# Sixteen chunk sums of a modulation vector, moved from a Hyena block into the attention's projections

## What is computed

```python
sh1, sc1, g1, sh2, sc2, g2 = jnp.split((silu(c) @ w_mod + b_mod), 6)          # 6 x 1024 numbers
csh1, csc1, ...            = jnp.split((silu(c_ctx) @ w_mod + b_mod), 6)      # only csh1, csc1 are used
h  = modulate(rms_norm(x, norm1_g), sh1, sc1)       # 1024 positions
hc = modulate(rms_norm(ctx, norm1_g), csh1, csc1)   # 256 positions
y  = token_mixers(h, hc, ...)     # Hyena, attention A (4 heads), differential attention D (4 heads), output projection
x  = x + g1 * y
h  = modulate(rms_norm(x, norm2_g), sh2, sc2)
x  = x + g2 * conv_glu(h, ...)
```

## Time and profile before

| what | value |
|---|---|
| runs (3) | 4012.69, 4017.70, 4017.53 us; median 4017.53 |
| profiled execution, its own time | 4013.59 us |
| span of its trace | 4012.3 us, so 1.3 us lie around it |
| TensorE busy, mean granted clock | 3562.4 us (89%), 0.965 |
| VectorE busy | 1372.2 us (34%) |
| ScalarE busy | 904.3 us (23%) |
| GpSimd busy | 245.5 us (6%) |
| first block's Hyena | about 181 to 443 us of the span |
| attention's projections | about 444 to 774 us |
| moved by DMA | 362.23 MB, mean 90 GB/s |

### The profile page before, as it was taken

How to read it: one execution, slowest core, us unless ns; L and a number is a source line. 1 busy time by engine, 2 the same in 40 slices (tenths; PEclk the granted TensorE clock), 3 DMA queues, 4 the chain that set the end, 5 groups by cost and what they waited for, 6 DMA issues and landing times.

```text
span 4012.3 us, 30603 instructions
## 1 busy us (share of the span) xinstructions
PE 3562.4 (89%) x12486; PEld 1958.2 (49%) x12486; DVE 1372.2 (34%) x2502; ACT 904.3 (23%) x1725; POOL 245.5 (6%) x236
## 2 busy tenths in 40 slices
PE   8797799888888899999999999999789978999991
PEld 4356454766664344444444456665356434444440
DVE  6758344166661211111100013224556141111116
ACT  1210245256662200000000012112334131111112
POOL 0002001000000000000000000000000002222213
PEclk9898999999999999999999999999999988999996
DMA  4225200000002111011011100002000118888874
GB/s 176 74 99 205 84 23 30 22 1 1 1 1 84 42 42 42 32 42 39 29 36 36 62 32 27 32 10 84 11 1 22 44 49 333 330 329 329 332 291 152
DMA packets 59784, 362.23 MB, mean 90 GB/s; under 512 B 6442, under 2 KB 12858, under 8 KB 33020
## 3 DMA queue, kind: packets, MB, share of 16 engines
q1 hardware_dynamic: 37036, 179.39, 12.3%
q0 software_dynamic: 22608, 180.89, 12.2%
HBM read 325.03 MB, written 35.22 MB: 90 GB/s over the span
## 4 chain that ended last, share of the span: by engine, by line
PE 75%; DVE 14%; ACT 8%; issue 2%; DMA 1%; POOL 0%; SPq 0%; DVEq 0%; ACTq 0%; POOLq 0%
PE ps L1154 15%; PE ps L2245 8%; PE ps L1201 8%; PE ps L1310 5%; PE ps L2262 4%; PE ps L764 4%; ACT arena L961 3%; PE ps L1904 3%; PE ps L1099 3%; PE ps L1312 3%; PE ps L664 2%; PE ps L767 2%; ACT arena L953 2%; PE ps L603 1%; PE ps L1744 1%
## 5 line engine op out<-in xcount | busy, mean ns | idle before, releaser
L1154 PE MATMUL ps<-arena 128*128 128x512 f32 x1408 | 606.3, 593 | 5.0 <-ACT arena L1140 5.0
L1154 PEld LDWEIGHTS ps<-arena 128*128 128x128 f32 x1408 | 268.1, 190 | 343.0 <-issue 337.3
L2245 PE MATMUL ps<-arena 128*128 128x512 f32 x752 | 332.0, 594 | 0.0
L1201 PE MATMUL ps<-arena 128*128 128x512 f32 x704 | 302.4, 591 | 1.4 <-DVE arena L1187 1.4
L2203 POOL DMA_INDIRECT arena<-in_wgu_dram,arena x47 | 44.2, 940 | 2837.7 <-DVE arena L2164 2593.0
L2245 PEld LDWEIGHTS ps<-arena 128*128 128x128 f32 x752 | 139.7, 191 | 159.1 <-issue 159.1
L2262 PE MATMUL ps<-arena 128*128 128x512 f32 x376 | 174.0, 605 | 48.6 <-DVE arena L2313 48.6
L1201 PEld LDWEIGHTS ps<-arena 128*128 128x128 f32 x704 | 132.8, 189 | 171.0 <-issue 168.8
L1310 PE MATMUL ps<-arena 128*128 128x512 f32 x480 | 210.6, 599 | 0.0
L764 PE MATMUL ps<-arena 128*128 128x512 f32 (+1 forms) x432 | 174.8, 558 | 7.8 <-DMA arena<-in_win_a_dram 7.8
L911 PE MATMUL ps<-arena 128*128 128x128 f32 x1280 | 163.1, 283 | 5.4 <-ACT arena L953 2.5
(11 more groups left out here) (331 smaller groups left out, 4697.3 us busy)
## 6 DMA issues: line engine op xcount, KB each, us to landing
arena<-in_wmod_dram SPq DMA_DIRECT2D x24, 1024.0 KB, 4.9
yslot<-arena SPq DMA_DIRECT2D x47, 512.0 KB, 7.8
arena<-in_wup_dram SPq DMA_DIRECT2D x22, 1024.0 KB, 4.9
arena<-in_wout_dram SPq DMA_DIRECT2D x16, 1024.0 KB, 4.8
arena<-in_cf_dram SPq DMA_DIRECT2D x12, 1024.0 KB, 5.0
arena<-in_wdn_dram SPq DMA_DIRECT2D x16, 704.0 KB, 4.1
arena<-in_w2b_dram SPq DMA_DIRECT2D x9, 1024.0 KB, 5.0
arena<-in_ci_dram SPq DMA_DIRECT2D x8, 1024.0 KB, 6.9
```

Source lines behind the costliest of these rows:

```text
L1154: ins = mm(bk(b + tc), sb(wat(n) + k * 256 + which * 128, 128), sb(HT + k * 1024 + tc * 512, 512), k == 0, k == 7)
L1201: ins = mm(bk(bs[tc]), sb(wat(n) + k * 128, 128), sb(GB + (11 * hh + k) * 1024 + tc * 512, 512), hh == 0 and k == 0, hh == 1 and k == 10)
L2245: ins = mm(bk(b), sb(XB + i % 2 * 1024 + k * 128, 128), sb(WGU[i % 3] + k * 512, 512), k == 0, k == 7)
```

## The change

Three things: the 16 late chunks leave the ring of weights, and get a buffer `WM` of 1 MB with a semaphore `lmod`; the calls of the three steps leave Hyena and stand in the loop over the 57 jobs, with their sums behind iteration i for i in `mod_at`, TensorE's step two iterations later and the bias three later; and `AMUL2` is made behind that loop. `WM` lies on memory that Hyena's transforms use, so its first load waits for Hyena's end. TensorE's step uses PSUM bank 7 for these chunks.

```diff
-WLIST = ([("cz", 1), ("wmod", 4)] + [("cf", 1), ("wmod", 1)] * 4 + [("win_hy", 1), ("wmod", 1), ("win_hy", 1), ("wmod", 2), ("win_hy", 1), ("wmod", 2)]
-         + [("cf", 1), ("wmod", 1)] * 4 + [("ci", 1), ("wmod", 1)] * 4 + [("cf", 1), ("wmod", 1)] * 3 + [("cf", 1)] + [("ci", 4)]
+WLIST = ([("cz", 1), ("wmod", 4)] + [("cf", 1), ("wmod", 1)] * 4 + [("win_hy", 3)]
+         + [("cf", 4), ("ci", 4)] * 2
...
+    WM = BIG + 31168
+    lmod = nc.alloc_semaphore("late_mod")
+    def mbank_of(i):
+        return 6 if i < 8 else 7
...
     def dve_mod_sums(i):
-        n = nth["wmod"][i]
+        w = wat(nth["wmod"][i]) if i < 8 else WM
         V.wait_ge(*(yield ("silu",)))
-        V.wait_ge(*wready(n))
+        V.wait_ge(*(wready(nth["wmod"][i]) if i < 8 else (lmod, 16 * (i - 7))))
...
-        at[("macc", i)] = at[("w", n)] = V.last()
+        at[("macc", i)] = V.last()
+        if i < 8:
+            at[("w", nth["wmod"][i])] = V.last()
...
     def pe_conv(o):
...
-            if (o, kt) < (1, 3):
-                yield from pe_mod_step(5 + 8 * o + kt)
...
-            if o == 0:
-                yield from pe_mod_step(9 + t)
...
     def dve_conv(o):
...
-            if (o, kt) < (1, 3):
-                yield from dve_mod_step(5 + 8 * o + kt)
...
-            if o == 0:
-                yield from dve_mod_step(9 + t)
...
     def pe_hyena():
...
                 yield from pe_hy_turn(f - 1)
-                yield from pe_mod_step(f - 1)
...
-        yield from pe_mod_step(16)
...
     def dve_hyena():
...
-            if f:
-                yield from dve_mod_step(f - 1)
         for o in range(2):
             yield from dve_conv(o)
-        yield from dve_mod_step(16)
...
+    mod_at = [4, 8, 12, 16, 20, 24, 28, 32, 36, 39, 42, 45, 48, 51, 53, 55]
     def sp_qkv():
         S.wait_ge(*(yield ("convd", 1, 3, 1)))
         LD.ready()
         dma.dma_start(out=sb(ROPE, 2048), in_=X["rope"]).then_inc(*LD.turn(("rope",)))
-        yield from sp_weights(nth["win_a"][0], nth["wout"][4])
+        yield from sp_weights(nth["win_a"][0], nth["win_d"][2])
+        n = nth["win_d"][2]
+        for i in range(8, 24):
+            if i > 8:
+                S.wait_ge(*(yield ("macc", i - 1)))
+            else:
+                S.wait_ge(*(yield ("convd", 1, 3, 1)))
+            dma.dma_start(out=sb(WM, 2048), in_=X["wmod"][i]).then_inc(lmod, 16)
+            if i in (8, 12, 13, 14, 15, 16, 20, 23):
+                yield from sp_weights(n, n + 1)
+                n += 1
     def pe_qkv():
...
+            if i - 2 in mod_at:
+                yield from pe_mod_sum(8 + mod_at.index(i - 2))
...
     def dve_qkv():
...
+            if i - 3 in mod_at:
+                yield from dve_mod_bias(8 + mod_at.index(i - 3))
+            if i in mod_at:
+                yield from dve_mod_sums(8 + mod_at.index(i))
+        vdone()
+        vt.tensor_scalar(sb(AMUL2, 8), modv[:, 4, :, 0], 1.0, None, ADD).then_inc(*V.step())
+        vdone()
+        vt.tensor_tensor(sb(AMUL2, 8), sb(AMUL2, 8), par("g2n"), MUL).then_inc(*V.step(("am2",)))
```

More of the change, by code:

```diff
@@ L243, in pe_mod_sum @@
     def pe_mod_sum(i):
-        nj = two[i]
-        yield from claim(6)
+        nj, b = two[i], mbank_of(i)
+        yield from claim(b)
         P.wait_ge(*(yield ("cons",)))
@@ L249, in pe_mod_sum @@
             for j in range(nj):
-                ins = mm(bk(6, 1, off=nj * c + j), sb(macc[i] + j * 256 + c * 128, 128), con("ones")[:, 0:1], True, True)
+                ins = mm(bk(b, 1, off=nj * c + j), sb(macc[i] + j * 256 + c * 128, 128), con("ones")[:, 0:1], True, True)
         ins.then_inc(*P.step(("modp", i)))
-        held[6] = [("mod", i)]
+        held[b] = [("mod", i)]
     def dve_mod_bias(i):
@@ L259, in dve_mod_bias @@
         V.wait_ge(*(yield ("modp", i)))
-        vt.tensor_tensor(to, bk(6, 2 * nj).rearrange("p (a j) -> p a j", j=nj), b, ADD).then_inc(*V.step(("mod", i)))
+        vt.tensor_tensor(to, bk(mbank_of(i), 2 * nj).rearrange("p (a j) -> p a j", j=nj), b, ADD).then_inc(*V.step(("mod", i)))
     def dve_mod_sums(i):
-        n = nth["wmod"][i]
+        w = wat(nth["wmod"][i]) if i < 8 else WM
         V.wait_ge(*(yield ("silu",)))
-        V.wait_ge(*wready(n))
+        V.wait_ge(*(wready(nth["wmod"][i]) if i < 8 else (lmod, 16 * (i - 7))))
         if i in before:
@@ L270, in dve_mod_sums @@
             a = sb(macc[i] + j * 256, 256)
-            vt.tensor_scalar(a, sb(wat(n), 256), sc[:, 0, j:j + 1], None, MUL).then_inc(*V.step())
+            vt.tensor_scalar(a, sb(w, 256), sc[:, 0, j:j + 1], None, MUL).then_inc(*V.step())
             for k in range(1, 8):
                 vdone()
-                vt.scalar_tensor_tensor(a, sb(wat(n) + k * 256, 256), sc[:, k, j:j + 1], a, MUL, ADD).then_inc(*V.step())
-        at[("macc", i)] = at[("w", n)] = V.last()
+                vt.scalar_tensor_tensor(a, sb(w + k * 256, 256), sc[:, k, j:j + 1], a, MUL, ADD).then_inc(*V.step())
+        at[("macc", i)] = V.last()
+        if i < 8:
+            at[("w", nth["wmod"][i])] = V.last()
     def act_rsqrt(y, x, ready, done):
@@ L556, in build @@
     yh = sb(YH, 2048).rearrange("p (j c) -> p j c", j=8)
[L558 to L566, removed]
     def pe_hy_turn(f):
```

## The result

| | before | after |
|---|---|---|
| median (13 runs each) | 4014.26 us | 4025.02 us |
| ratio | 1 | 1.0026, 95% interval 1.0017 to 1.0034 |
| profiled execution: span | 4012.3 us | 4022.8 us |
| first projection of Hyena to first load of `win_a` | 262.42 us | 239.85 us |
| first load of `win_a` to the first scores ("the stage" below) | 330.74 us | 367.52 us |

The change makes the kernel 10.8 us slower. Hyena gives 22.6 us, the stage of the projections takes 36.8. Hyena's 239.85 us are of one profiled execution.

What follows compares the result with a forecast made beforehand. TensorE bounds most of the kernel (75% of the chain), VectorE Hyena's first forward transform. -26.0 + 21.8 + 2.1 + 3.0 = +0.9, taken as +1 us: 4018.5 us on a median of 4017.5, no tellable change 68%, range 4009 to 4032.

Steps and rivals of the forecast that it cites:

- What is taken out: Hyena without the late chunks: gain 26.0 us, 23.8 in forward transforms plus 2.2 for TensorE's steps; bounds 23 to 27.
- The six turns: Three chunks in each of Hyena's two forward transforms stand on the path: 6 x 3.97 = 23.8 us gained.
- What is put in: Attention's projections with the late chunks: 21.8 us, plus 2.1 for GpSimd and 3.0 for the clock; range 20.5 to 33.
- chunk 9's wait: At value job 10 TensorE would stand from 526.6 until chunk 9's sums end at 529.0: 2.4 us new.
- chunk 16's stall: Before the last key job TensorE already waits 1.59 us, so all 3.90 is added; the stall becomes 5.5 us.
- TensorE's clock: Slower TensorE records behind the grown stalls at chunks 13 and 16: 1.5 us each, 3.0 in all; bounds 0 and 6.
- GpSimd beside the sums: Sums of chunks 8, 12, 13 and 16 meet GpSimd's rotation product: 0.53 us each, 2.1 in all; bounds 0 and 5.1.
- The first: Rival: waits behind chunks 13, 15 and 16 take in their stalls, so 14 us faster, 4003 us; 10%.
- The second: Rival: with landings of 7 us, loads and sums through one buffer bound the value jobs from chunk 16: 4034 us; 10%.
- The third: Rival: six sums in query and key jobs cost full length plus 1.5 us of clock each, 23 slower, 4041 us; 7%.
- The fourth: Rival: TensorE at half rate in Hyena's forward turns eats most of the gain, some 20 us slower, 4038 us; 5%.
- the ten other chunks in Hyena: Their sums run while VectorE would wait for TensorE or ScalarE anyway, so removing those sums gains nothing.

Runs made afterwards that it cites:

- none: The changed kernel without its sixteen late chunks (no loads, sums, TensorE steps or biases, 0.5 in place of their results): 3989.2 us, ratio 0.9939 to before.
- nocontact: The changed kernel with GpSimd's rotation product cut to one column for jobs 3, 19, 23, 27 and 35: 4019.0 us.
- twobuf: The changed kernel with a second chunk buffer, so a load need not wait for the previous chunk's sums: 4026.0 us.
- half: The changed kernel with three of seven multiply-adds per late chunk, same places, loads and steps: 4007.0 us.
- value: The changed kernel with two chunk buffers and the late chunks' sums in value jobs alone: 3996.2 us.
- hy_drop6: The kernel before without the six chunks behind turns 0 to 2 of both forward transforms in Hyena: 3993.7 us.
- fill: The changed kernel with 19 extra matmuls in front of TensorE's waits in iterations 10, 26, 28, 34 and 38: 4019.6 us.
- drop_qk: The changed kernel without the six chunks summed between query and key jobs (8, 12 to 16): 3999.2 us.
- value_one: The changed kernel with sums in value jobs alone, but with its one chunk buffer: 4048.4 us.
- hy_drop10: The kernel before without the other ten late chunks of Hyena, the six behind the forward turns kept: 4013.1 us.

## Why the forecast was too low, though its range held

The forecast was +1 us with 68% for a change of under 8 us; it was +10.8. So by its own measure of 8 us the forecast missed, and the side that came, slower by over 0.2%, had 22%. The range (4009 to 4032) holds the 4025.0, but not by its working: the change cost 36.8 us where the bounds were 20.5 to 33, and the net of +10.8 lies just outside -6 to +10. Two things held it, of which either was enough: the 2 us added for spread, and a base of three runs (4017.5) that lay 3.3 us above the median of thirteen. That is luck. The balance was right in its shape (a gain in Hyena of a little over 20, and a loss in the projections of more). Two terms of the loss were mis-sized.

*What is taken out.* The six turns gave what the working says: forward transforms of 35.13 and 39.38 us, against 47.08 and 51.34 before, so 11.95 and 11.96 (forecast 11.9 each; the first is counted from VectorE's first instruction in it, the second from TensorE's). TensorE's steps gave 2.9 in place of 2.2 (1.4 at the projections, 1.5 at the first inverse transform). Still the whole of Hyena gave 22.6 in place of 26.0, as three places took 4.1 us longer: the first two projections 30.56 in place of 29.17 us, the first records of the first transform 1.3 more, and the second inverse transform 30.82 in place of 29.39. At the first and the third of them the granted clock was 0.91 and not 0.95. This was not in the sum. But some 2.2 to 2.7 us of it are not the change's: the five kernels with the shorter Hyena (none, nocontact, twobuf, half, value) started what follows these projections 28.9 to 29.3 us after Hyena's first, where after took 30.40, and in them Hyena was 24.7 to 25.3 us shorter than before. Counted so, before took 29.01 us, and hy_drop6, the same kernel up to there but for one memset, 30.53. What stays in all of them is the longer second inverse transform.

*What is put in.* The lateness of after against before, counted from the first projection (426.02 and 451.03) at the same jobs:

| stretch | forecast | measured |
|---|---|---|
| to value job 9 (chunk 8) | 1.9 + 0.5 | 3.0 |
| value jobs 9 to 16 (chunks 9, 10) | 4.3 | 7.0 |
| jobs 17 to 24 (steps of 11 and 12) | 2.0 + 0.5 | 3.2 |
| jobs 25 to 28 (chunk 13) | 3.6 + 0.5 + 1.5 | 7.2 |
| jobs 29 to 32 (chunk 14) | 0.4 | 0.8 |
| jobs 33 to 36 (chunk 15) | 2.3 | 4.0 |
| jobs 37, 38 (chunk 16) | 4.3 + 0.5 + 1.5 | 6.5 |
| value jobs to the first scores | 3.6 | 5.1 |
| sum | 27.4 | 36.8 |

(Forecasts with a plus name the meeting with GpSimd and the clock apart. The terms of the prediction add up to 22.4 and not to the 21.8 that it gives, a slip of 0.6 us in the adding, which made the forecast +0.9 where its own terms give +1.5.)

The terms of the prediction have a second slip, of 0.4 us: 523.6 + 1.9 + 3.90 is 529.4 and not 529.0, so that chunk 9's wait would be 2.8. Neither slip decides anything.

The working of the waits held well: chunk 16's stall was to be 1.59 + 3.90 + the meeting, and was 6.50; the stalls of chunks 12 and 15 were to grow to 1.2 and to 2.36 + 1.9, and were 2.03 (with its meeting) and 4.25; chunk 9's was to be 2.4, and was 2.7. The terms that failed are the two "of which the rows show only relatives":

- **TensorE's clock**, taken as 3.0 us for two stalls, with a bound of 6. The split by none leaves 10.7 us beyond waits and steps; fill shows that much of this lies behind the stalls (10.20, 8.99 and 2.04 us back to 7.39, 7.11 and 1.10). The error was to count only the stalls of chunks 13 and 16, and 1.5 us each: the wait for chunk 9 alone, of 2.7 us, was followed by 2.8 us of loss, which covered the time in which chunk 10's wait would have been. It did not have to be so: in drop_qk a wait of 2.59 us at this place cost nothing behind it.
- **GpSimd beside the sums**, taken as 0.53 us from line 621 at four meetings. It is 0.9 to 1.0, at five. After's rows and nocontact show it. The rule of the Trainium skill (SBUF — State Buffer, "SBUF: two separate sides"), the loser fully blocks, comes nearer than the neighbouring line did: GpSimd's product takes 1.27 us, and the sum that met it grew by nearly that. Line 621 was the wrong relative. It stands beside a product of half the width (0.96 us) that had started before it, which may be why it lost less; no run tests this.

The rivals. The first (room larger than counted) is out: waits grew by 17 us. The second (the single buffer) is out for this placement (twobuf), and its mechanism is real (value_one). The third (sums at full length, and the clock with each) is the nearest: its clock half happened, its other half did not, as the stretches of chunks 12, 14 and 15 cost 3.2, 0.8 and 4.0 us and not 6.7. The fourth is out: forward turns took 8.06 us. That the ten other chunks in Hyena are nearly free was a step of the working, and hy_drop10 shows it (1.9 us).

What stays open: why the second inverse transform of Hyena has more of the lower clock now (30.82 us, and 30.66 without any chunk, at 0.91) than before (29.39 us, at 0.95), though its gap ahead is shorter now, 8.16 against 12.15 us; and why a wait lowers the clock at one place and not at another. No run was made on that.

## What to carry to other kernels

Work moved away from a bounding engine costs, in its new place, what exceeds the helper engine's slack at that very instruction, not in the stage's average: with two buffers, the same sixteen sums cost the stage 35.4 us where six of them lie between query and key jobs (twobuf), and 8.5 us where all lie in value jobs (value). Each stall that they make on TensorE is to be counted with what it does to the records behind it, here half as much again as the added waits (10.7 against 19.4 us). And work that is gathered in one gap can need a second buffer, even if the spread-out version does without.

## What the runs showed of the hardware that was not expected

- Waits of the same length leave TensorE's clock alone at one place and lower it at another: four waits of 2.35 to 2.37 us in the kernel without chunks were followed by a projection of 8.50 us, two of 7.03, and a value job of 4.21 (3.61 at full rate). In half, a wait of 2.09 was followed by 8.49. Behind chunk 9, 2.68 us cost 2.8 in after and 2.59 cost nothing in drop_qk. So a loss of this kind can be bounded from the rows, not placed. TensorE's timeline of none:

```profile
606.21 1.39 PE L768 MATMUL ps<-arena 128*128 128x512 f32 x2 [2.36 <-DVE arena L813]
...
607.39 8.50 PE L747 MATMUL ps<-arena 128*128 128x512 f32 x16
...
631.59 1.12 PE L768 MATMUL ps<-arena 128*128 128x512 f32 x2 [2.36 <-DVE arena L813]
...
632.56 7.03 PE L747 MATMUL ps<-arena 128*128 128x512 f32 x16
...
678.97 2.08 PE L768 MATMUL ps<-arena 128*128 128x512 f32 x2 [2.37 <-DVE arena L813]
...
680.84 4.21 PE L750 MATMUL ps<-arena 128*128 128x256 f32 x16
```

- Filling a stall with matmuls brought the records behind it to full rate (7.39 in place of 10.20 us at a granted clock of 1.00 in place of 0.71). With 16 us more work on TensorE the stage was 4.0 us shorter.
- VectorE's `tensor_scalar` with one input in SBUF was held up by GpSimd's product as much as the seven-step sums were: 1.38 us instead of 0.35, and 0.35 again in nocontact. Where the product met the seven steps, they took 0.9 to 1.1 us longer in all, not each.
